# Low-part score products on 64 of the 128 rows in a two-layer encoder trunk

## What is computed

```python
# layer 0: 8 heads, two maps c of 64 dimensions each
s = jnp.einsum('bqhcd,bkhcd->bhcqk', qx, k) * scale
p = jax.nn.softmax(s, axis=-1)
a = p[:, :, 0] - lam * p[:, :, 1]
# layer 1: keys of the block, one before and one after, |i-j| <= 128
s = jnp.einsum('bqhgd,bkhd->bhgqk', qx, kx) * scale
```

## Time and profile before

| | us |
|---|---|
| median of three runs | 1152.68 |
| span of the profiled execution | 1149.1 |
| TensorE busy (products) | 1123.6 |
| TensorE weight loads busy | 912.9 |
| VectorE busy | 975.0 |
| ScalarE busy | 677.8 |

### The profile page before, as it was taken

How to read it: one execution, slowest core, us unless ns; L and a number is a source line. 1 busy time by engine, 2 the same in 40 slices (tenths; PEclk the granted TensorE clock), 3 DMA queues, 4 the chain that set the end, 5 groups by cost and what they waited for, 6 DMA issues and landing times. The chain is left out here.

```text
span 1149.1 us, 18542 instructions
## 1 busy us (share of the span) xinstructions
PE 1123.6 (98%) x5752; PEld 912.9 (79%) x5752; DVE 975.0 (85%) x1925; ACT 677.8 (59%) x1326; POOL 0.2 (0%) x4
## 2 busy tenths in 40 slices
PE   7999999999999999999999999999999999999996
PEld 6778778778778778778878867887888888888876
DVE  6889889889889889889889898888888888888886
ACT  6475564564554654654654665366666566666664
POOL 0000000000000000000000000000000000000000
PEclk9999999999999999999999999999999999999999
DMA  7614323323224224224125121545232324323111
GB/s 224 165 37 126 113 74 87 97 73 95 88 73 102 80 73 117 65 73 124 59 73 138 47 74 31 122 129 142 61 91 55 91 68 120 98 63 91 55 38 74
DMA packets 131531, 103.62 MB, mean 90 GB/s; under 512 B 5408, under 2 KB 116384, under 8 KB 131488
## 3 DMA queue, kind: packets, MB, share of 16 engines
q1 hardware_dynamic: 131344, 102.81, 32.5%
q10 hardware_dynamic: 144, 0.26, 0.1%
HBM read 77.88 MB, written 2.10 MB: 70 GB/s over the span
## 5 line engine op out<-in xcount | busy, mean ns | idle before, releaser
L74 PE MATMUL bank_proj<-hH,w_hi 128*128 128x512 f32 x856 | 343.0, 401 | 1.2 <-issue 0.8
L76 PE MATMUL bank_proj<-hH,w_lo 128*128 128x512 f32 x856 | 334.8, 391 | 0.0
L75 PE MATMUL bank_proj<-hL,w_hi 128*128 128x512 f32 x856 | 334.5, 391 | 0.0
L76 PEld LDWEIGHTS bank_proj<-hH,w_lo 128*128 128x128 f32 x856 | 161.0, 188 | 35.3
L74 PEld LDWEIGHTS bank_proj<-hH,w_hi 128*128 128x128 f32 x856 | 161.6, 189 | 32.7 <-issue 1.2
L75 PEld LDWEIGHTS bank_proj<-hL,w_hi 128*128 128x128 f32 x856 | 161.6, 189 | 30.6 <-issue 0.2
L2012 ACT ACTIVATE probs<-bank_odd_score,small 128x256 f32<-128x256 f32 (+1 forms) x128 | 66.3, 525 | 73.0 <-DVE small L2263 73.0
L1253 DVE TENSOR_TENSOR w_lo<-w_raw,w_hi 128x1024 fp32r<-128x1024 f32 x74 | 89.6, 1218 | 0.8 <-ACT w_hi L741 0.7
L2019 ACT ACTIVATE probsT<-bank_odd_turn 128x256 fp32r<-128x256 f32 (+1 forms) x128 | 48.8, 434 | 62.8 <-PE bank_odd_turn L1733 62.7
L741 ACT ACTIVATE w_hi<-w_raw 128x1024 fp32r<-128x1024 f32 x74 | 77.9, 1053 | 0.2
L806 ACT ACTIVATE probs<-bank_score,small 128x512 f32<-128x512 f32 x64 | 43.4, 684 | 55.1 <-DVE small L1091 49.3
(11 more groups left out here) (452 smaller groups left out, 2218.8 us busy)
## 6 DMA issues: line engine op xcount, KB each, us to landing
w_raw<-in_w_in_even SPq DMA_DIRECT2D x72, 512.0 KB, 4.7
w_raw<-in_w_in_odd SPq DMA_DIRECT2D x36, 512.0 KB, 4.2
qs<-parts SPq DMA_DIRECT2D x96, 128.0 KB, 2.3
ks<-parts SPq DMA_DIRECT2D x40, 256.0 KB, 4.3
o_raw<-in_w_out_even SPq DMA_DIRECT2D x15, 512.0 KB, 6.1
o_raw<-in_w_out_odd SPq DMA_DIRECT2D x14, 512.0 KB, 6.6
mixT<-in_x SPq DMA_DIRECT2D x2, 512.0 KB, 5.9
attT<-in_x SPq DMA_DIRECT2D x2, 512.0 KB, 6.7
```

The source lines that it names most:

```text
L74: pe.matmul(out, hi, moving_hi, start=start, stop=False)
L75: pe.matmul(out, hi, moving_lo, start=False, stop=False)
L76: return pe.matmul(out, lo, moving_hi, start=False, stop=stop)
```

## The change

In both layers the transfers put the second map's (or head's) queries the other way round: high part on rows 64 to 127, low part on rows 0 to 63. The high product of the 128 rows is the same sum as before. The low product takes only the 64 rows on which the high part of the queries lies: rows 0 to 63 for the first map or head, 64 to 127 for the second. The product of the two low parts is no longer in the sum. Both low products now stand at the end of a score step, behind both high ones and, in the second layer, behind the bands, and raise `full` there. In the second layer the key head is handed down as the number `group` instead of being worked out from `h`.

```diff
@@ move_q, first layer
                     for part in range(2):
-                        sp.dma_start(qs[HD * part:HD * part + HD, c, :].bitcast(F32),
+                        to = HD * (part ^ c)
+                        sp.dma_start(qs[to:to + HD, c, :].bitcast(F32),
                                      parts[HD * c:HD * c + HD, part, :].bitcast(F32)).then_inc(q_moved.sem, DMA)
@@ scores, first layer
                     pe.matmul(S[c][:], qs[:, c, t * P:(t + 1) * P], ks[:, c, 0, :], start=True, stop=False)
-                    pe.matmul(S[c][:], qs[:, c, t * P:(t + 1) * P], ks[:, c, 1, :], start=False,
+                for c in range(2):
+                    rows = slice(HD * c, HD * c + HD)
+                    pe.matmul(S[c][:], qs[rows, c, t * P:(t + 1) * P], ks[rows, c, 1, :], start=False,
                               stop=True).then_inc(S[c].full.sem, 1)
@@ move_q, second layer
-                        sp.dma_start(qs[HD * i:HD * i + HD, half, c, :].bitcast(F32),
+                        to = HD * (i ^ c)
+                        sp.dma_start(qs[to:to + HD, half, c, :].bitcast(F32),
@@ scores, second layer
-            def scores(h, half, t):
+            def scores(h, half, t, group):
...
+                keys = lambda part, rows: ks[rows, (2 * (2 * half + group) + part) * SEQ + lo * P:
+                                             (2 * (2 * half + group) + part) * SEQ + (lo + n) * P]
                 for a in range(2):
                     if S[a].free.due(h, tile_use(half, t) - 1):
                         pe.wait_ge(S[a].free.sem, S[a].free.at(h, tile_use(half, t) - 1))
-                    at, query = S[a][:, 0:n * P], qs[:, half, a, t * P:(t + 1) * P]
-                    for part in range(2):
-                        keys = ks[:, bass.ds((2 * key_head(h, half) + part) * SEQ + lo * P, n * P)]
-                        mm = pe.matmul(at, query, keys, start=part == 0, stop=False)
+                    pe.matmul(S[a][:, 0:n * P], qs[:, half, a, t * P:(t + 1) * P], keys(0, slice(0, P)),
+                              start=True, stop=False)
                     if t > 0:
-                        mm = pe.matmul(S[a][:, 0:P], eye_b[:], band[:, 0], start=False, stop=t == NC - 1)
+                        pe.matmul(S[a][:, 0:P], eye_b[:], band[:, 0], start=False, stop=False)
                     if t < NC - 1:
-                        mm = pe.matmul(S[a][:, (n - 1) * P:n * P], eye_b[:], band[:, 1], start=False, stop=True)
-                    mm.then_inc(S[a].full.sem, 1)
+                        pe.matmul(S[a][:, (n - 1) * P:n * P], eye_b[:], band[:, 1], start=False, stop=False)
+                for a in range(2):
+                    rows = slice(HD * a, HD * a + HD)
+                    pe.matmul(S[a][:, 0:n * P], qs[rows, half, a, t * P:(t + 1) * P], keys(1, rows),
+                              start=False, stop=True).then_inc(S[a].full.sem, 1)
```

More of the change, by code:

```diff
@@ L1573, in slot @@
             return (n + 5) % 3 if n <= 0 else (n + 2) % SLOTS
-        def key_head(h, half):
-            return 2 * half + h // 4
         def window(t):
@@ L1790, in first_head @@
                 pe.wait_ge(k_moved.sem, k_moved.at(0, 4))
-                scores(0, 0, 0)
+                scores(0, 0, 0, 0)
                 proj(0, 0, 3)
@@ L1794, in first_head @@
                 turns(0, 0, 0)
-                scores(0, 0, 1)
+                scores(0, 0, 1, 0)
                 proj(0, 1, 0, 4)
@@ L1798, in first_head @@
                 turns(0, 0, 1)
-                scores(0, 0, 2)
+                scores(0, 0, 2, 0)
                 proj(0, 1, 4)
@@ L1802, in first_head @@
                 turns(0, 0, 2)
-                scores(0, 0, 3)
+                scores(0, 0, 3, 0)
                 proj(0, 2, 0, 5)
@@ L1808, in first_head @@
                 pe.wait_ge(k_moved.sem, k_moved.at(0, 8))
-                scores(0, 1, 0)
+                scores(0, 1, 0, 0)
                 proj(0, 2, 5)
@@ L1813, in first_head @@
                 turns(0, 1, 0)
-                scores(0, 1, 1)
+                scores(0, 1, 1, 0)
                 turn_weight(0, 0, turn_of(1, False))
@@ L1818, in first_head @@
                 turns(0, 1, 1)
-                scores(0, 1, 2)
+                scores(0, 1, 2, 0)
                 proj(0, 4, 0, 4)
@@ L1822, in first_head @@
                 turns(0, 1, 2)
-                scores(0, 1, 3)
+                scores(0, 1, 3, 0)
                 proj(0, 4, 4)
@@ L1831, in half_step @@
                 turns(h_before, before, 3)
-                scores(h, half, 0)
+                scores(h, half, 0, group)
                 proj(h, n, 0, 4)
@@ L1836, in half_step @@
                 turns(h, half, 0)
-                scores(h, half, 1)
+                scores(h, half, 1, group)
                 turn_weight(h_before, before, turn_of(half, True))
@@ L1842, in half_step @@
                 turns(h, half, 1)
-                scores(h, half, 2)
+                scores(h, half, 2, group)
                 out_tile(h, 4 * half)
@@ L1847, in half_step @@
                 turns(h, half, 2)
-                scores(h, half, 3)
+                scores(h, half, 3, group)
                 out_tile(h, 4 * half + 2)
@@ L1941, in _ @@
             turns(HEADS - 1, 0, 3)
-            scores(HEADS - 1, 1, 0)
+            scores(HEADS - 1, 1, 0, 1)
             late_tile(4, W, 4)
@@ L1946, in _ @@
             turns(HEADS - 1, 1, 0)
-            scores(HEADS - 1, 1, 1)
+            scores(HEADS - 1, 1, 1, 1)
             turn_weight(HEADS - 1, 0, 5)
@@ L1951, in _ @@
             turns(HEADS - 1, 1, 1)
-            scores(HEADS - 1, 1, 2)
+            scores(HEADS - 1, 1, 2, 1)
             late_tile(7, W, 6)
@@ L1957, in _ @@
             turns(HEADS - 1, 1, 2)
-            scores(HEADS - 1, 1, 3)
+            scores(HEADS - 1, 1, 3, 1)
             open_two(1, 0)
```

## The result

The changed kernel took 1168.48 us (median of four runs, 1166.84 to 1168.94), the kernel before 1152.04 us on the same chip: ratio 1.0145, 95% interval 1.0131 to 1.0159, so +16.7 us (0.0145 of 1152). The forecast was +7.0. The direction was right and the time lies in the range, but the change is 2.4 times the one that was forecast.

What follows compares the result with a forecast made beforehand. TensorE's stream of columns was taken to bound the kernel. Terms -16.6 + 16.6 + 5.3 + 1.1 + 0.6 = +7.0 us gave a span of 1156.1, plus 3.6 to the runs' median: 1159.7 us, range 1141 to 1182.

Steps and rivals of the forecast that it cites:

- What bounds the kernel: Whole kernel: TensorE's stream of columns sets the end, so time taken from or given to it counts nearly in full.
- The gain of the pairs: Score steps, both layers: two low products stream side by side, one of each of 96 pairs free, 16.6 us at most.
- The change of shape: Around each pair: 192 changes between 128 and 64 rows, each exposing one load, together 16.6 us.
- The upper bound: At changes of shape: the array also runs empty, 0.16 us lost 192 times, another 31 us.
- rival B: At each change of shape the array empties, 0.08 to 0.16 us: +22 to +38 us, 1175 to 1190; chance 0.22.
- The second load of the pair: Inside each pair: the second load starts 0.11 us late if in sequence, 10.6 us; half taken, 5.3 us.
- What the order moves: Layer one's last score step: unfilled wait for the second bank, 1.1 us, and VectorE's later start, 0.6 us.
- VectorE's later start: Layer one's last score step: reduction 0.34 us later, lengthening TensorE's wait at the residual's addition, 0.6 us in all.
- TensorE's wait for ScalarE at 227 us: Last score step of a layer-one pass, second high load: the wait grows by 0.2 us.
- A: Changes of shape are free, loads made ahead, pairs side by side: -12.6 us, 1140.1, or 1150.7 with sequential loads; chance 0.31.
- C: Pairs don't run side by side: 1171 with exposed loads, 1155 with free changes of shape; chance 0.11.
- Slower: Whole kernel: the changed kernel measures slower than before, beyond the 0.2% (2.3 us) that can be told; chance 0.59.

Runs made afterwards that it cites:

- experiment 2: Changed kernel with both low products of a pair on the same rows 0 to 63: 1181.01 us, ratio 1.0255 to the kernel before.
- experiment 6: Changed kernel with the high products on 64 rows too and the queries' low part left out, two pairs in a row: 1153.69 us, ratio 1.0007 to before.
- experiments 3 and 4: Changed kernel with 64-row products in the first layer only, then the second only, the other layer 128 rows in changed order: 1159.77 and 1165.24 us.
- experiment 1: Changed kernel with both low products on all 128 rows again, in the changed order: 1156.32 us, ratio 1.0036 to the kernel before.

## Why the prediction was right and wrong

**What bounds the kernel: right in the main.** TensorE's stream set the end, and in the second layer 9.6 of the 12.5 us that the steps lost reached the end of the kernel (0.34 us for both changes of a step, so 10.9 + 10.9 - 9.3 saved). In the first 3.8 of about 5.8 did (64 x 0.205 - 7.3). The rest went into waits, which "nearly in full" had left too little room for.

**The gain of the pairs, 16.6 us at most: right.** They start 3 ns apart, and taking the different rows away cost 12.7 us, of which layer two had all that was expected (experiment 2), 8 x 1.18 = 9.4 us.

**The change of shape, 16.6 us: the term that failed.** It was sized by one exposed load, 0.11 us. The load is exposed as forecast, but 0.10 us of emptying come on top, in both directions: 0.21 us each. The upper bound had the emptying at 0.16 us, and rival B had its half, 0.08, as its lower end; B, given 0.22, is what happened, at a price between its ends. By the records the term is 64 x 0.205 = 13.1 us in the first layer and 10.9 + 10.9 in the second, 35 us instead of 16.6. The 18 us between them are 192 x 0.095: the exposed loads were counted rightly, and what failed is the emptying, left out of the sum. (B's time, 1175 and more, was not reached, since it carried the 5.3 us of the next term and no waits given back.) The step of it that was wrong was the choice: that the load held back between the kinds of weights was the nearest row. In those rows the array does not change its shape, so they could not show an emptying; they bounded the term from below and no more. The sentence on the Trainium skill's page "TensorEngine Tiling (Array Packing)", Key Properties, said that a change of mode drains TensorE and that tiles of one mode work in parallel: the trace agrees with both, with 0.10 us a change beside it, and a place in one mode costs nothing (experiment 6).

**The second load of the pair, +5.3 us: wrong, it is 0.** Two loads on different rows run side by side (230.28, x2 in 0.19 us). The 0.11 us of the earlier trace rows holds for loads on the same rows (experiment 2: x2 in 0.29 us).

**What the order moves, 1.1 + 0.6 us: right place, too small.** The order alone cost 4.1 us. Of its cost 0.2 us a pass, some 1.8 in all, is at the place named, the 0.227 of the prediction; the 0.1 a pass of layer two and what lies outside the loops were not in the sum, and were not taken apart further. That VectorE's later start would keep TensorE waiting at the output tiles was right: the wait of 0.34 us is 0.39 in the changed kernel, although TensorE comes later.

**Where errors met.** -16.6 for the pairs, +35 for the changes of shape, 0 for the loads, +4.1 for the order make +22.5; measured is +16.7. The rest, about 6 us, is what the waits gave back: 2 us in the first and 3 in the second layer by experiments 3 and 4, the last one inside the intervals. So the forecast missed by 10 us and not by more through luck: 18 us too little for the shape and 2.4 for the order met 5.3 too much for the loads and some 6 us of waits given back that the sum did not have. The range held the time because it took in the lower part of rival B. The forecast that TensorE's wait for ScalarE at 227 us would grow by 0.2 us failed by the same. With the order alone it did: the load's wait went from 0.37 to 0.48 and 0.17 us of idle TensorE came on top (experiment 1). With the changes of shape it is 0.27 (229.85): TensorE comes later to a softmax whose time it does not set. (ScalarE waits for VectorE before it, 4.24 us at 228.35.)

**The rivals.** A (changes of shape free) is out by every record. C (no side by side) is out by experiment 2. Slower had 0.59. Its ground, that two changes cost as much as a stream saves, was right in kind and too weak: they cost about twice as much or more, 0.41, 0.34 and 0.34 us against 0.227, 0.173 and 0.118.

## What to carry to other kernels

Half-height products side by side pay where many of them stand in a row: here one pair saved 0.12 to 0.23 us, and the way in and out cost 0.3 to 0.4. Count the changes of the array's shape before the rows saved, and where a cost has no row, do not take a price from rows that lack its cause. Products with another kind of weights took less of TensorE's time in one group than in several (0.07 us a step for the bands, at the end or in the middle); half or more of it went into a wait behind, and only the bands at the end left a gain that can be told (-0.1 to -0.2%).

## What the runs showed of the hardware

A change between products of 128 and of 64 rows cost 0.20 to 0.21 us each way: 0.09 to 0.10 us without any stream, and a load of fp32 weights (0.11 us) not made ahead. Where a bf16 band had left part of a load open before, the two changes together cost 0.34 us. With bf16 weights the empty time was the same, 0.09 to 0.10 us (one size, 128 columns). Two products on different halves of the rows started 3 ns apart, their loads too, and pairs followed each other at the price of one stream (0.23 us). Not expected was that the emptying is the same on the way in and out and does not depend on the kind of weights; and that a TensorE with 98% busy time still got back a third of the loss in the first layer from waits of a few tenths of a microsecond.
